# Late attention with four pairs of map buffers: scores and maxima three units ahead of the turning, not two

## The reference, cut to what matters

```python
s = jnp.einsum("bqhcd,bkhcd->bhcqk", qb, k).astype(jnp.float32) * scale
s = jnp.where(mask, s, -jnp.inf)
p = jax.nn.softmax(s, axis=-1)
w = (p[:, :, 0] - lam * p[:, :, 1]).astype(v.dtype)
return jnp.einsum("bhqk,bkhe->bqhe", w, v)
```

## Time and profile before

| what | value |
| --- | --- |
| median of three runs | 3068.22 us |
| profiled execution, its own time | 3068.41 us |
| its span | 3066.6 us |
| TensorE busy, whole span | 94% |
| the stage of the change, first layer, 1833 to 1976 us | TensorE 105.94 of 143 us |
| the same in the second layer, 2513 to 2656 us | TensorE 107.55 of 143 us |
| granted clock in the stage | 0.81 and 0.80 |

### The profile page before, as it was taken

How to read it: one execution, slowest core, us unless ns; L and a number is a source line. 1 busy time by engine, 2 the same in 40 slices (tenths; PEclk the granted TensorE clock), 3 DMA queues, 4 the chain that set the end, 5 groups by cost and what they waited for, 6 DMA issues and landing times.

```text
span 3066.6 us, 38125 instructions
## 1 busy us (share of the span) xinstructions
PE 2897.8 (94%) x14517; PEld 2352.9 (77%) x14517; DVE 1084.6 (35%) x2075; ACT 722.7 (24%) x1775; POOL 1643.5 (54%) x1719
## 2 busy tenths in 40 slices
PE   6999999999999899999999897799999988799999
PEld 3545878888878799999999764488888764588887
DVE  1036643313255200000001238447274148357272
ACT  3136752101110111111110223332022213332020
POOL 0121037767777310107783444478787644478786
PEclk8999999999999799999999998899999988899999
DMA  6260013233432399999999302332333203133321
GB/s 184 68 189 15 15 30 100 93 102 93 149 109 83 102 247 263 264 261 273 295 301 306 101 31 73 104 87 95 100 93 112 73 32 127 57 94 97 99 93 52
DMA packets 543188, 388.03 MB, mean 127 GB/s; under 512 B 31178, under 2 KB 493221, under 8 KB 542488
## 3 DMA queue, kind: packets, MB, share of 16 engines
q1 hardware_dynamic: 523728, 327.85, 37.6%
q0 software_dynamic: 12832, 41.22, 4.0%
q10 hardware_dynamic: 6440, 16.44, 1.5%
HBM read 345.12 MB, written 40.80 MB: 126 GB/s over the span
## 4 chain that ended last, share of the span: by engine, by line
PE 87%; DVE 5%; ACT 3%; issue 2%; DMA 1%; POOL 1%; SPq 1%; ACTq 1%; another core or an unknown queue 0%; DVEq 0%; POOLq 0%
PE bank L579 17%; PE bank L581 17%; PE bank L580 17%; PE bank L736 15%; PE bank L1148 6%; PE bank L826 2%; PE bank L804 2%; PE bank L1222 1%; PE bank L1230 1%; PE bank L814 1%; PE bank L790 1%; PE bank L776 1%; DMA ring<-in_moe_w_up 1%; SPq L1352 1%; ACT x_hi L1501 1%
## 5 line engine op out<-in xcount | busy, mean ns | idle before, releaser
L1914 POOL TENSOR_TENSOR unit_parts<-ring,unit_parts 128x512 fp32r<-128x512 f32 x580 | 804.2, 1387 | 48.4
L1912 POOL TENSOR_SCALAR unit_parts<-ring 128x512 fp32r<-128x512 f32 x580 | 425.3, 733 | 452.5 <-PE bank L581 320.8
L579 PE MATMUL bank<-x_hi,unit_parts 128*128 128x512 f32 x1408 | 557.1, 396 | 16.9 <-DVE x L2370 10.3
L581 PE MATMUL bank<-x_hi,unit_parts 128*128 128x512 f32 x1408 | 550.5, 391 | 0.0
L580 PE MATMUL bank<-x_lo,unit_parts 128*128 128x512 f32 x1408 | 550.1, 391 | 0.0
L736 PE MATMUL bank<-arena,ring 128*128 128x160 f32 x2816 | 389.8, 301 | 8.9 <-DMA ring<-in_moe_w_up 5.5
L736 PEld LDWEIGHTS bank<-arena,ring 128*128 128x128 f32 x2816 | 387.5, 192 | 9.5 <-DMA ring<-in_moe_w_up 5.8
L579 PEld LDWEIGHTS bank<-x_hi,unit_parts 128*128 128x128 f32 x1408 | 265.8, 189 | 75.9 <-DVE x L2370 11.5
L579 PE MATMUL bank<-unit_parts,hid_parts 128*128 128x512 f32 x784 | 307.9, 393 | 2.6 <-DVE hid_parts L2392 2.6
L580 PEld LDWEIGHTS bank<-x_lo,unit_parts 128*128 128x128 f32 x1408 | 265.9, 189 | 57.5 <-issue 2.9
L581 PEld LDWEIGHTS bank<-x_hi,unit_parts 128*128 128x128 f32 x1408 | 265.6, 189 | 55.7
(11 more groups left out here) (330 smaller groups left out, 3663.1 us busy)
## 6 DMA issues: line engine op xcount, KB each, us to landing
ring<-in_moe_w_gate SPq DMA_DIRECT2D x88, 512.0 KB, 6.6
ring<-in_moe_w_up SPq DMA_DIRECT2D x88, 512.0 KB, 7.3
ring<-in_moe_w_down SPq DMA_DIRECT2D x64, 704.0 KB, 5.2
ring<-in_w_up SPq DMA_DIRECT2D x88, 512.0 KB, 5.0
ring<-in_w_down SPq DMA_DIRECT2D x16, 1024.0 KB, 5.0
ring<-in_od_w_in SPq DMA_DIRECT2D x24, 512.0 KB, 4.8
s_stream<-arena POOLq DMA_DIRECT2D x12, 1024.0 KB, 9.2
arena<-s_stream SPq DMA_DIRECT2D x16, 768.0 KB, 4.2
```

The lines of the kernel that those rows point to most:

```text
L579: pe.matmul(ps, a[0], b[0], start=start, stop=False)
L581: return pe.matmul(ps, a[1], b[0], start=False, stop=stop)
L1912: pool.tensor_scalar(hi, raw, 1.0, 1.0, ALU.mult, ALU.mult).then_inc(S("units_rounded"), 1)
L1914: pool.tensor_tensor(lo, raw, hi.bitcast(F32), ALU.subtract).then_inc(S("units_split"), 1)
```

## The change

A fourth pair of buffers is added to `late_p` (unit m uses pair m mod 4). All engines put scores, maxima and exponentials of unit i + 3 in step i, where they had those of i + 2. The other steps of a unit keep their place, so ratio and scale of unit m still stand in step m - 1 and its turning in step m. The steps begin at -3 and are dealt to the rounds anew by `LATE_AT`. VectorE waits for the turning of unit m - 4 before it writes a map, and before a ratio it waits for the drained values of unit m - 4.

```diff
-LATE_AT = (-2, 0, 2, 4, 6, 8, 10, 11, 12)
+LATE_AT = (-3, -1, 1, 3, 5, 7, 9, 11, 12)
...
-        late_p = region(SCR, 6, T)
+        late_p = [region(SCR + T * i, T) for i in range(6)] + [region(21760 + T * i, T) for i in range(2)]
...
                 def attend(i):
-                    if i + 2 < UNITS_LATE:
-                        score(i + 2)
+                    if i + 3 < UNITS_LATE:
+                        score(i + 3)
...
-                    if i + 2 < UNITS_LATE:
-                        probs(i + 2)
+                    if i + 3 < UNITS_LATE:
+                        probs(i + 3)
...
-                for i in range(-2, 13):
+                for i in range(-3, 13):
                     attend(i)
...
-                    if m >= 3:
-                        wait_filled(dve, ("T2", l, m - 3))
+                    if m >= 4:
+                        wait_filled(dve, ("T2", l, m - 4))
...
                     dve.wait_ge(S("late_probs"), 2 * (UNITS_LATE * l + m) + 2)
+                    if m >= 4:
+                        wait_drained(dve, ("O2", l, m - 4))
...
-                    if i + 2 < UNITS_LATE:
-                        maxima(i + 2)
+                    if i + 3 < UNITS_LATE:
+                        maxima(i + 3)
```

More of the change, by code:

```diff
@@ L1248, in turn_probs @@
                     for kt in range(m % NT + 1):
-                        ins = pe.transpose(ps[:, kt * P:(kt + 1) * P], late_p[:, 2 * (m % 3), kt * P:(kt + 1) * P],
+                        ins = pe.transpose(ps[:, kt * P:(kt + 1) * P], late_p[2 * (m % 4)][:, kt * P:(kt + 1) * P],
                                            c("ident"))
@@ L1788, in probs @@
                         n = P * (m % NT + 1)
-                        s_, at = 2 * (m % 3) + cc, 2 * (m % 4) + cc
-                        act.activation(late_p[:, s_, 0:n], late_p[:, s_, 0:n], ACT.Exp, scale=-1.0,
+                        s_, at = 2 * (m % 4) + cc, 2 * (m % 4) + cc
+                        act.activation(late_p[s_][:, 0:n], late_p[s_][:, 0:n], ACT.Exp, scale=-1.0,
                                        bias=nmx[:, at:at + 1], accum_out=psumsum[:, at:at + 1])\
@@ L1796, in scale_map @@
                     n = P * (m % NT + 1)
-                    s_, at = 2 * (m % 3) + 1, 2 * (m % 4) + 1
+                    s_, at = 2 * (m % 4) + 1, 2 * (m % 4) + 1
                     act.wait_ge(S("ratio_ready"), UNITS_LATE * l + m + 1)
-                    act.activation(late_p[:, s_, 0:n], late_p[:, s_, 0:n], ACT.Copy, scale=coef[:, at:at + 1])\
+                    act.activation(late_p[s_][:, 0:n], late_p[s_][:, 0:n], ACT.Copy, scale=coef[:, at:at + 1])\
                        .then_inc(S("map_scaled"), 1)
@@ L2150, in merge_maps @@
                     pool.wait_ge(S("map_scaled"), UNITS_LATE * l + m + 1)
-                    a, b = (late_p[:, 2 * (m % 3) + cc, 0:n] for cc in range(2))
+                    a, b = (late_p[2 * (m % 4) + cc][:, 0:n] for cc in range(2))
                     pool.tensor_tensor(a, a, b, ALU.add).then_inc(S("maps_merged"), 1)
@@ L2712, in maxima @@
                         ps = wait_filled(dve, key)
-                        drain(dve.tensor_tensor_reduce(out=late_p[:, 2 * (m % 3) + cc, 0:n], in0=ps[:, 0:n],
+                        drain(dve.tensor_tensor_reduce(out=late_p[2 * (m % 4) + cc][:, 0:n], in0=ps[:, 0:n],
                                                        in1=c("bandd")[:, T - n:T], scale=1.0, scalar=3e38, op0=ALU.add,
```

## The result

| kernel | median | runs | ratio of runs to before, 95% |
| --- | --- | --- | --- |
| before | 3067.77 us | 3064.84 to 3077.43 (19) | |
| changed | 3075.36 us | 3070.94 to 3079.19 (19) | 1.0022 (1.0015 to 1.0029) |

The change makes the kernel slower, by 0.22%, some 7 us: just past the 0.2% that I had called no change, inside the stated range, and 6 us above the forecast of 3069.4. The profiled execution has a span of 3077.4 us.

What follows compares the result with a forecast made beforehand. TensorE, busy 94% of the span, bounds the kernel except in the two late-attention stages. The terms -1.7 - 0.2 - 2.6 + 3.9 + 1.5 - 0.5 + 0.2 give +0.6 us a layer: 3069.4 us, range 3061 to 3077.

Steps and rivals of the forecast that it cites:

- The first rival: The turns' waits for the merge go, 19.4 us in all, giving 3049; chance 0.04.
- The second sign: Sign of being wrong, in the rounds: more than one round changes its clock.
- step 9: Round 7 and tail: larger scores +0.4 and +0.5, no exponentials in step 13 -1.4; sum -0.5 us a layer.
- Step 3: Rounds 0 to 2, less work in front: -2.2 us on TensorE, about -1.7 left at round 3's start.
- Steps 1 and 4: Each round's first merge smaller, 0.4 us a round; round 3 with a longer last values product, -0.2 in sum.
- Step 2: Second merges smaller in rounds 3 and 5, larger in 2 and 4; -0.6 us for round 4, none for others.
- The rival: Second merges, by the lock rule: a 512-column merge stops a scan for its length, about 1.3 us in two rounds.
- Steps 5 and 6: subln(0) moves from round 3 to round 4, ahead of turn_out; round 4 -2.6 us, lead 4.5 at round 5.
- Step 7: Round 5: rest_late(4) now ahead of turn_out(5) and add_y(4); +3.9 us, between +2.5 and +4.5.
- Step 8: Round 6: two steps for one, subln(1) ahead of turn_out(6), add_y(5) and values(9) ahead of state_out(6); +1.5 us.
- Step 10: New waits, for the turning of m - 4 and ahead of the ratio: 0.2 us a layer, 0 to 1.2.
- the slower one: Round 5's stall not paid by a lead, if lead there is under 1.5 us; +3.6 a layer, 3076; chance 0.20.

Runs made afterwards that it cites:

- The experiment: The changed kernel with subln(0) and subln(1) one step later, in steps 6 and 10, behind turn_out: 3071.11 us, ratio 1.0009.

## Why the prediction was right, and where not

The measured 3075.4 us lies in the stated range of 3061 to 3077, near its upper end, and the range was wide. The most likely outcome, no change, was missed by 1 us, and slower had been given 0.20. The mechanism was right in most steps; the number is inside owing to the bounds put on the stall and the clock.

**The stages and the merge's waits.** Right. The waits of the turns for the merge did not go: 3.10, 2.56, 0.86 and 4.21 us in rounds 1 to 4, 10.7 us, where I had said over 6. The first rival (they go) is out. The ratio never waited for exponentials, which was the first sign of being wrong. The second sign, a changed clock in more than one round, did come: beside state_in of round 3, state_out(6) and (7), the gate product and the output product changed (step 9).

**Step 3, less in front.** Right in sign, -1.6 for -2.2 at round 2, and the same -1.4 for -1.7 at round 3. What became late next I had not seen. The chain of the changed kernel, ahead of round 2's state_in:

```profile
1863.14 0.32 SPq L1367
1863.46 0.04 issue
1863.51 4.79 DMA cst<-s_stream
1868.29 0.04 issue
1868.33 0.70 PE bank L1222
```

The tables of group 3 are fetched when state_out(0) is done, and land 4.8 us later. State_in now comes early enough to meet the transfer, so no further gain could be had there while the tables are fetched at that point.

**Steps 1 and 4, the smaller merges and round 3.** -0.2 forecast, +0.3 measured, and so the lead at round 4 was 1.1 us, not 1.9. The clock carries it: state_in of round 3 took 5.0 us in one profile of the changed kernel and 3.5 in the other, and the lead at round 4 was 0.4 us in the first and 1.9 in the second.

**Step 2, the second merges.** Half right. Merge 3 in round 2 (512 columns) meets scan(3) and takes 2.17 us; no state_in waited for it, as said. Merge 5 does not come clear of its scan, it takes 1.68 us beside L2679. The rival had the larger merges stop a scan for their length. None did so in the changed kernel: beside the three merges of 512 columns in the rounds (2.17 us each) and beside this one L2679 took 1.20 us, free. No scan of the stage was stretched, where four were before (1.41 to 1.95 us). The loser was GpSimd:

```profile
1896.89 1.20 DVE L2679 TENSOR_TENSOR_SCAN xnT<-s5small,xnT 128x512 f32<-128x512 f32 x1
...
1896.92 1.68 POOL L2152 TENSOR_TENSOR arena<-arena 128x256 f32<-128x256 f32 x1 [3.79 <-ACT arena L1799]
```

That the two exclude each other stands. Who goes first is the earlier one here (the scan by 0.03 us), in the earlier trace rows and in the kernel with subln moved, where the merge of 512 columns did stop the scan (2.22 us). But in round 4 the merge started 0.24 us ahead of L2688 and still lost to it and the two behind it. What decides there is open.

**Steps 5 and 6, subln(0) and round 4.** -2.8 measured, -2.6 forecast. But I costed subln on VectorE, where it is cheap, and not on GpSimd, where it holds the merge. The experiment says 1.0 us in round 4. One reading of the old trace was too narrow: I took the two layers as alike, with state_in of round 4 at the high clock. In the second layer before it took 4.4 us at 0.61, with a round as long as in the first (15.4 us); in the changed kernel it took 2.7 us in all four instances.

**Step 7, rest_late ahead of turn_out.** The place and the price are right: 3.1 us from ratio to L2688, and the turn waits for add_y. Round 5 grew by 4.5 us, forecast +3.9, bound +4.5. With tile 4 one step later 3.2 us of it went, and in the old kernel the same stall alone made 3.9.

**Step 8, round 6.** +1.5 forecast and +1.5 measured. Its cause was mostly the held merge: with subln out of the way the round is 1.7 us shorter. Subln's own length on VectorE isn't in it, since turn_out(6) was done (1935.90) some 2 us before state_out(6) began (1937.99).

**Step 9, the tail: the term that was mis-sized.** -0.5 forecast, +0.1 measured (round 7 -0.6, o7 to the gate +1.5, gate to the output -0.8). The missing exponentials are as read: no L1790 stands between L1417 and L1799, and they gave the 1.4 us forecast (0.8, plus the 0.6 that the gate product is longer). What the sum lacked is the clock. State_out(7) takes 5.3 us for 4.3, all at 1.2 GHz, behind a wait of 4.95 us for 4.61. And the gate product takes 6.0 us at a mean clock of 0.62, for the 5.4 before; I had this only as a risk, of 1.8 us. In round 7 the clock gave 1.2 us back: state_out(6), which no longer waits 4.3 us for L2691, takes 4.1 us for 5.3. The windows of state_out(6) before and after, then of the other two after, then of the four state_in for the earlier trace rows:

```profile
1931.26:1936.55 5.29, 5.29 (x8) 1.89 (x8) 2.70 (x3) 0.00 (x0) 1.26 (x1) 0.53 0.00 0
1937.99:1942.10 4.11, 4.11 (x9) 1.56 (x8) 1.77 (x2) 1.56 (x5) 3.39 (x2) 0.66 0.03 6
```
```profile
1949.60:1954.90 5.30, 5.28 (x8) 0.54 0.00 0
1963.50:1969.50 6.00, 5.96 (x8) 0.62 0.00 0
```
```profile
1881.70:1886.50 4.80, 4.80 (x8) 0.53 0.00 0
1895.30:1898.00 2.70, 2.70 (x9) 1.00 0.00 0
1907.90:1911.60 3.70, 3.70 (x8) 0.71 0.00 0
1924.30:1928.40 4.10, 4.10 (x9) 0.65 1.05 388
```

**Step 10, the waits.** 0.2 forecast; with buffers and waits alone the stages took 138.4 us both, no cost shown.

**The sum.** +2.2 us a layer for +0.6. The difference of 1.6 us is made of the lead at round 3 (0.3), round 3 (0.5), round 5 (0.6) and the tail (0.6), less 0.2 each for round 4 and the new waits. Two steps turned their sign: round 3 (-0.2 forecast, +0.3 measured) and the tail (-0.5, +0.1), both in part by the clock. Behind the stages come 0.65 us a layer in the output product, a term that the sum put at nothing. Of the rivals the slower one had the right sign, and its 3076 lies nearest, but its condition was not met: the lead at round 5 was 3.9 us, far over 1.5. The result is the forecast's mechanism with round 5 at its upper bound and the clock against it. The chance of 0.20 for slower was too low: the price of the stall was read from a row, while most gains were estimates.

## What to carry to other kernels

Where an engine's queue is written out by hand, a step that waits for another engine must stand behind the work that the next round needs, and a shift of the schedule moves every such step with it: list them before shifting anything. Here the deeper buffer brought nothing that could be shown, while moving two roundings and two scalings behind turn_out took 15 us off the changed kernel, and moving one rounding took 6 us off the kernel before. A row of the old trace at a place where the pattern already stands (round 7: 3.0 us) gave the price of the stall in the changed kernel to 0.1 us (3.5 us in the old one), and also pointed to the cure.

## What was not expected of the hardware

- VectorE's back-to-back products can keep GpSimd out: a merge of 384 columns took 0.99 us alone, 1.32 us with one product beside it, 2.98 us when subln and three products ran through, and one of 512 columns 3.15 us. Without subln ahead the two went in turns. That subln makes the difference is a guess from two kernels.
- One order of instructions gives state_in of round 3 as 3.4 or as 4.8 us in the two layers of one execution, and as 3.5 or 5.0 in two executions. Stages of one kernel differed by up to 3 us (137.4 and 134.4), not all of it by this.
